# Gathering the first expert's 32 rows alone, and the other 96 rows of its group in its down phase

## The reference, cut to what matters

```python
def expert_choice_moe(h, w_router, w_gate, w_up, w_down):
    cap = EC_CAPACITY_FACTOR * length // N_EXPERTS          # 2 * 256 // 16 = 32
    aff = jax.nn.softmax((h @ w_router).astype(jnp.float32), axis=-1)
    gate, idx = lax.top_k(jnp.swapaxes(aff, 1, 2), cap)
    xe = h[bidx, idx]
    hid = jax.nn.silu(jnp.einsum("becd,edf->becf", xe, w_gate)) * jnp.einsum("becd,edf->becf", xe, w_up)
    ye = jnp.einsum("becf,efd->becd", hid, w_down) * gate[..., None].astype(h.dtype)
    return jnp.zeros_like(h).at[bidx, idx].add(ye)
```

## Time and profile before

| what | us |
|---|---|
| median of 3 runs | 1738.16 |
| the profiled execution | 1738.64 |
| its span in the profile | 1736.5 |
| TensorE busy (matmul records) | 1573.5 |
| VectorE busy | 854.9 |
| ScalarE busy | 678.7 |
| data moved | 431.90 MB |

### The profile page before, as it was taken

One profiled execution on the slowest core, in us unless ns is written; L12 is line 12 of the kernel. 1 busy time (PEld: TensorE's weight loads), 2 busy tenths in 40 slices (PEclk: granted clock), 3 DMA queues, 4 the chain that ended last, 5 costly groups with the idle time before them and its releaser, 6 DMA issues.

```text
span 1736.5 us, 31676 instructions
## 1 busy us (share of the span) xinstructions
PE 1573.5 (91%) x13753; PEld 1335.3 (77%) x13761; DVE 854.9 (49%) x1166; ACT 678.7 (39%) x904; POOL 0.2 (0%) x4
## 2 busy tenths in 40 slices
PE   8999989999999999999999999999998866756765
PEld 7999976999999999879999889897884422422422
DVE  6556796765676666766656567956220000000001
ACT  5444535644454445455444556667221100100101
POOL 0000000000000000000000000000000000000000
PEclk9999999999999999999999999999999988987978
DMA  8755588665656555636555433347759999999997
GB/s 293 257 193 193 170 248 261 233 202 176 200 163 204 200 188 168 208 104 199 195 190 167 146 107 113 111 157 283 268 207 414 425 426 426 426 428 427 426 427 319
DMA packets 193902, 431.90 MB, mean 249 GB/s; under 512 B 8387, under 2 KB 150901, under 8 KB 178708
## 3 DMA queue, kind: packets, MB, share of 16 engines
q1 hardware_dynamic: 187540, 422.19, 66.7%
q10 hardware_dynamic: 6272, 8.39, 1.5%
HBM read 428.62 MB, written 1.93 MB: 248 GB/s over the span
## 4 chain that ended last, share of the span: by engine, by line
PE 68%; DMA 22%; DVE 6%; ACT 3%; issue 1%; another core or an unknown queue 0%; ACTq 0%; DVEq 0%
PE banks L812 14%; PE banks L813 14%; PE banks L814 14%; DMA arena<-in_w_exp_down 5%; DMA xn<-in_w_exp_up 3%; DMA ring<-in_w_exp_gate 3%; DMA h<-in_w_exp_down 3%; DMA squares<-in_w_exp_gate 3%; DMA arena<-in_w_exp_up 3%; DMA ring<-in_w_exp_up 2%; PE banks L1292 2%; PE banks L1294 2%; PE banks L1293 2%; PE banks L1437 2%; PE banks L1567 2%; PE banks L1471 2%
## 5 line engine op out<-in xcount | busy, mean ns | idle before, releaser
L812 PE MATMUL banks<-x_split,w_split 128*128 128x256 f32 x1600 | 446.7, 279 | 7.2 <-DVE w_split L2233 4.6
L2233 DVE TENSOR_TENSOR w_split<-ring,w_split 128x1024 fp32r<-128x1024 f32 x288 | 346.0, 1224 | 199.2 <-ACT w_split L1659 198.8
L814 PE MATMUL banks<-x_split,w_split 128*128 128x256 f32 x1600 | 442.7, 277 | 0.0
L813 PE MATMUL banks<-x_split,w_split 128*128 128x256 f32 x1600 | 442.7, 277 | 0.0
L1659 ACT ACTIVATE w_split<-ring 128x1024 fp32r<-128x1024 f32 x287 | 295.0, 1052 | 151.0 <-PE banks L814 149.0
L812 PEld LDWEIGHTS banks<-x_split,w_split 128*128 128x128 f32 x1600 | 301.3, 188 | 9.7 <-issue 4.4
L813 PEld LDWEIGHTS banks<-x_split,w_split 128*128 128x128 f32 x1600 | 301.2, 188 | 0.4
L814 PEld LDWEIGHTS banks<-x_split,w_split 128*128 128x128 f32 x1600 | 301.1, 188 | 0.0
L812 PE MATMUL banks<-hid_split,w_split 128*128 128x256 f32 x704 | 194.8, 277 | 1.8 <-DVE hid_split L2310 1.8
L813 PE MATMUL banks<-hid_split,w_split 128*128 128x256 f32 x704 | 194.3, 276 | 0.0
L814 PE MATMUL banks<-hid_split,w_split 128*128 128x256 f32 x704 | 194.3, 276 | 0.0
(11 more groups left out here) (490 smaller groups left out, 2275.1 us busy)
## 6 DMA issues: line engine op xcount, KB each, us to landing
ring<-in_ffn_w SPq DMA_DIRECT2D x131, 1024.0 KB, 5.3
arena<-in_w_exp_gate SPq DMA_DIRECT2D x13, 2048.0 KB, 45.4
arena<-in_w_exp_down SPq DMA_DIRECT2D x12, 2048.0 KB, 45.1
arena<-in_w_exp_up SPq DMA_DIRECT2D x11, 2048.0 KB, 45.9
ring<-in_w_in SPq DMA_DIRECT2D x21, 1024.0 KB, 5.3
ring<-in_w_mod SPq DMA_DIRECT2D x20, 1024.0 KB, 5.2
ring<-in_w_exp_down SPq DMA_DIRECT2D x9, 2048.0 KB, 44.1
ring<-in_w_exp_gate SPq DMA_DIRECT2D x7, 2048.0 KB, 45.9
```

Of the source, the lines that this page charges most:

```text
L812: mm(out_, hi, moving(0), start=start, stop=False, **kw)
L813: mm(out_, hi, moving(1), start=False, stop=False, **kw)
L814: return mm(out_, lo, moving(0), start=False, stop=stop, **kw)
L2233: ins = dve.tensor_tensor(half_part(n, o, 1), half_slot(n, o, columns), half_part(n, o, 0).bitcast(F32), ALU.subtract)
```

## The change

The gathering of the first group is cut in two. Before the products of expert 0 only its own 32 columns of `picks` are the moving operand, and ScalarE takes 32 columns of each piece. The other 96 columns are gathered by `gather_group(0)` in the down phase of expert 0, between its second and third product, after `spread(1)`; ScalarE takes them in 8 activations after its copy of the turned hid of expert 0. The counts of the semaphores `x_exp_product` and `x_exp_taken` rise by 2 from there on: expert 1 waits for 6 rather than 4, and so on. The stationary operands and the number of matmuls of the first four pairs stay as they are.

```diff
+        def group_slots(group):
+            return slice(CAP if group == 0 else 0, GROUP * CAP)
...
-            def gather(k, bank, column):
-                o = ps[:, bank, column:column + GROUP * CAP]
+            def gather(k, bank, column, slots):
+                o = ps[:, bank, column + slots.start:column + slots.stop]
                 for t in range(TT):
                     w = tok[:, t, :].rearrange("p (j c i) -> p j i c", j=2, i=4)[:, k // 4, k % 4, :]
-                    last = mm(o, w, picks[:, t, :], start=(t == 0), stop=(t == TT - 1))
+                    last = mm(o, w, picks[:, t, slots], start=(t == 0), stop=(t == TT - 1))
...
-                    last = gather(k, 5 + j % 2, (k % 2) * P)
+                    last = gather(k, 5 + j % 2, (k % 2) * P, slice(0, CAP))
...
-                    last = gather(k, 4 + k // 4, (k % 4) * P)
+                    last = gather(k, 4 + k // 4, (k % 4) * P, group_slots(group))
...
-                    pe.wait_ge(sem("x_exp_taken"), 4 + 2 * group)
+                    pe.wait_ge(sem("x_exp_taken"), 4 + 2 * (group + 1))
...
                     if j == 2 and not final:
                         spread(e + 1)
-                        if e % GROUP == GROUP - 1:
+                        if e == 0:
+                            gather_group(0)
+                        elif e % GROUP == GROUP - 1:
                             gather_group(group + 1)
...
-            def modulated_rows(k, data):
-                return fn(x_exp[:, k, :], data, ACT.Identity, ...)
+            def modulated_rows(k, bank, column, slots):
+                return fn(x_exp[:, k, slots], ps[:, bank, column + slots.start:column + slots.stop], ACT.Identity, ...)
...
-                    ins = modulated_rows(k, ps[:, 5 + j % 2, (k % 2) * P:(k % 2) * P + P])
+                    ins = modulated_rows(k, 5 + j % 2, (k % 2) * P, slice(0, CAP))
...
-                if e % GROUP == GROUP - 1 and not final:
-                    group = e // GROUP + 1
+                if e == 0 or e % GROUP == GROUP - 1 and not final:
+                    group = 0 if e == 0 else e // GROUP + 1
...
-                    dve.wait_ge(sem("x_exp_product"), 4 + 2 * (e // GROUP))
+                    dve.wait_ge(sem("x_exp_product"), 4 + 2 * (e // GROUP + 1))
                     picked(e // GROUP + 1)
```

More of the change, by code:

```diff
@@ L2125, in _ @@
             fn(gate_rows, ps[:, 5, :], ACT.Copy).then_inc(sem("gate_rows_ready"), 1)
-            def modulated_rows(k, data):
-                return fn(x_exp[:, k, :], data, ACT.Identity, bias=pair_gain[:, 1, k:k + 1], scale=pair_gain[:, 0, k:k + 1])
+            def modulated_rows(k, bank, column, slots):
+                return fn(x_exp[:, k, slots], ps[:, bank, column + slots.start:column + slots.stop], ACT.Identity,
+                          bias=pair_gain[:, 1, k:k + 1], scale=pair_gain[:, 0, k:k + 1])
             def spread_of(e):
@@ L2148, in _ @@
                    ps[:, 7, 0:256].rearrange("p (i j s) -> p i j s", i=4, j=2), ACT.Copy).then_inc(sem("hid_t_ready"), 1)
-                if e % GROUP == GROUP - 1 and not final:
-                    group = e // GROUP + 1
+                if e == 0 or e % GROUP == GROUP - 1 and not final:
+                    group = 0 if e == 0 else e // GROUP + 1
                     for k in range(KD):
                         if k % 4 == 0:
-                            act.wait_ge(sem("x_exp_product"), 4 + 2 * (group - 1) + k // 4 + 1)
-                        ins = modulated_rows(k, ps[:, 4 + k // 4, (k % 4) * P:(k % 4) * P + P])
+                            act.wait_ge(sem("x_exp_product"), 4 + 2 * group + k // 4 + 1)
+                        ins = modulated_rows(k, 4 + k // 4, (k % 4) * P, group_slots(group))
                         if k % 4 == 3:
```

## The result

The changed kernel takes 1742.35 us (median of 12 runs, 1740.35 to 1744.61), the kernel before 1738.0 us (median of 12). The ratio is 1.0020, with a 95% interval of 1.0013 to 1.0027: 2.3 to 4.7 us slower (the medians differ by 4.35). The median lies above the stated range of 1735.3 to 1741.3, and the ratio's 3.5 us stand at the edge of what the prediction took as no change.

A forecast was written before the change was run, and what follows sets the result against it. The stream of expert weights was taken to bound the kernel. Tails -0.3, second gather +7.7, hidden -7.7, thin queue +0.5 gave +0.2 us on 1738.16: 1738.4 us, range 1735.3 to 1741.3.

The forecast's parts named there:

- What bounds the kernel: Experts: the stream of expert weights at its full rate sets the end; TensorE counts only by freeing buffers, releasing loads.
- Part 1, the record: First four pairs with 32 moving columns: 32 records remain at 0.237 us each, held by reading stepped weights.
- tails: Last record's moving columns at three places where a product follows a pair of gathers; 0.3 us saved in all.
- Rival A: First gathers: load and moving time add up, so fewer columns save 2.7 to 3.4 us plus tails; chance 0.14.
- Part 1, the clock: First four pairs: the forecast's -0.3 us holds no clock term; a later return to 2.4 GHz was a rival.
- rival C: Start of experts: clock returns to 2.4 GHz later, delaying the stream's start 1 to 2.5 us; chance 0.25.
- Part 2, the cover: Expert 0's down phase: the 96-column gather adds 7.7 us on TensorE, hidden by loads already issued.
- thin queue: Before pairs 32 and 34: few issued loads remain, priced from 0 to 1.0 us and taken as 0.5.
- Rival B: Before pair 34: queue runs dry if the clock is low after the second gather, 1742.4 us; chance 0.08.
- The sum: Whole kernel: -0.3 + 7.7 - 7.7 (hidden) + 0.5 = +0.2 us, giving 1738.4 us.
- the margin of 0.5 to 2 us: Pair 32, issued at 1325.0 after the second gather, meets its limit with 0.5 to 2 us to spare.
- the text's own drain: Issued loads before pair 32: 9.19 MB at 0.429 MB/us last to 1332.4, or 1327.5 without pair 32.

The follow-up runs named there:

- packed kernel: Kernel before, with ScalarE writing token rows so the 128 features of a gather's weights lie side by side; 1735.94 us, ratio 0.9986.
- part 1 alone: Changed kernel without the second gather and its 8 ScalarE activations, 32 columns gathered for expert 0; 1741.41 us, ratio 1.0015 to the kernel before.
- both gathers wide: Changed kernel, but first pairs and the gather in expert 0's down phase both use 128 moving columns; 1738.98 us, ratio 1.0001 to the kernel before.
- packed kernel with the change: Changed kernel, with token rows written so the gather's weights lie side by side; 1739.25 us, ratio 0.9999 to the kernel before.

## Why the prediction was wrong, step by step

**What bounds the kernel: right.** The stream of weights sets the end, and TensorE counts through its releases.

**Part 1, the record: right.** A record was to stay at 0.237 us. With 32 columns 16 records took 3.94 us and 8 took 2.01, and the weight loads 329 ns. The gain at the tails was 0.16 + 0.05 + 0.05, near the 0.3 taken. Rival A (load and moving time add up) asked for 2.6 us or less for the first 16 records, and falls by the 3.94. The packed kernel refutes its ground too: a record there takes 0.115 us with 128 moving columns, which alone need 0.111. The same holds against the row-group rule of the Trainium skill (TensorE: Matmul & The Clock Gate, The mechanism): these loads use all rows, and overlap with the matmuls in flight all the same. The rule of 16-byte lines of the Trainium skill (SBUF — State Buffer, Door 1: The DMA port swizzle) is borne out at a granted clock of 1.00, 328 against 192 ns for the same data.

**Part 1, the clock: this is the step that failed.** The forecast kept the clock of the row before, so its sum has no term for it, and set a later return of the clock aside as rival C with a chance of 0.25, priced at 1 to 2.5 us. It is what happened in all four profiles with 32 moving columns. The price was about right: part 1 alone costs 1.8 us by the figure and 2.6 measured. The forecast's sum had -0.3 for this part. The argument's own strong point should have been the warning: since the weight loads hold the record at 0.24 us, fewer columns can't shorten it, and so they only empty it. TensorE moves a quarter of the columns in the same time, while the rows had shown that the clock is low there even with 128 columns (0.50 in 1296.10 to 1298.10, 0.64 in 1298 to 1300). That the number of columns decides when the clock comes back is shown (one edit, 32 or 128 columns); that it does so through this emptiness is inferred.

**Part 2, the cover: right for the gather, wrong for what joined it.** The 7.7 us are covered, as the kernel with both gathers wide shows (+0.2 us). The forecast had +0.5 us for a thin queue and nothing for the clock behind the gather. Rival B named the place (before pair 34; it was pair 32 by a hair, 10.6 against 10.4) and the cause (the low clock over the down products), but with the chance 0.08, because expert 3's gather had kept its clock. That gather had 128 columns; this one has 96, and in both profiles with 96 columns and stepped weights the clock was 0.50 behind it, in all three with 128 it was 1.00. The edit from 96 to 128 alone (second gather wide) took the two down products from 3.62 to 1.90 us. The row taken as the nearest had the property that the change takes away.

**The sum: the cases don't exclude each other.** Forecast, B and C were given one chance each, as if only one could come. But the late start (19.2 us from the first gather to the end of the up tiles, 16.65 before), the second gather (7.7) and the slow down products (+1.7 for the pair) all delay the same pair 32, and the margin of 0.5 to 2 us was counted from the old start. What was free by itself (7.7) was paid for as soon as the others had used up the cover: pair 32's figure went from -1.5 to 10.6, of which only what lies above 6.9 costs. B was also priced too high in one term: its "+3.2" took the 1.92 and 3.54 us of the rows for one down product, where they are two together, so the low clock there costs 1.7. Its +1 for the scatter and +2 for the tiles behind it didn't come either: in the kernel after they take 1.99 and 7.09 us, as before. Joined, the text's own drain gives pair 32 at 1317.33 + 2.5 + 7.7 + 1.7 = 1329.2, its bytes 0.5 to 2 us later, and so 2.2 to 3.7 us after the 1327.5 at which the stream runs dry: 1738.16 + 2.2 to 3.7 = 1740.4 to 1741.9. The interval of the measured ratio, on the same 1738.16, is 1740.4 to 1742.9.

## What to carry to other kernels

Before columns are taken from a matmul, ask what holds its record; where it is the weight load, the cut saves next to nothing (0.26 us here), and the emptier engine may be granted the lower clock for the work behind it, as here. Where a stream of loads is the bound, write down for each load its issue time less the stream's time for the tiles ahead of it; only the greatest of these costs anything, and delays that lie ahead of the same load are added before they are compared with the cover. Rivals that act on the same load are one case together, not several with small chances.

## What the runs showed of the hardware

A float32 weight load of 128 columns that lie 4 elements apart takes 328 ns, and 0.24 us a record, at a granted clock of 1.00 and of 0.50 alike: 8 gather records took 2.06 us at 1.00 and 2.01 us at 0.50. The same columns side by side take 1.09 us for 8 records at 1.00, and 1.85 us at 0.50 in the packed kernel with the change; one load there is 192 ns long at 1.00 and 328 ns at 0.50. So the packed load goes by TensorE's clock, and the stepped one is held by something else. At the low clock the step costs next to nothing (2.01 against 1.85 us for 8 records). ScalarE reads PSUM with a step of 4 elements over 1024 columns in 1.11 us, as long as without the step (1.11 and 1.12 us in the kernel before).

In the start of the experts the granted clock fell to 0.50 within the first gather in all seven profiles with stepped weights. It came back to 1.00 by 1302 in each of the four with 128 moving columns, and was still 0.50 over 1302 to 1308 in all three with 32. With packed weights it stayed at 1.00 throughout with 128 columns and was 0.57 over 1302 to 1308 with 32. What the chip counts to decide this, these runs don't tell.
